# Router logits by held token columns, and three reorderings ahead of the experts

## What is computed

```python
def hierarchical_moe(h, rg_w, rg_b, re_w, re_b, e_gate, e_up, e_down):
    t = h.reshape(-1, D)
    g_prob = softmax(t @ rg_w + rg_b)                 # 4 groups
    g_val, g_idx = top_k(g_prob, 1)
    e_logits = (t @ re_w + re_b).reshape(-1, 4, 8)    # 8 experts in each group
    e_sel = take_along_axis(e_logits, g_idx)[:, 0]
    e_val, e_idx = top_k(softmax(e_sel), 2)
    ...
    for gi in range(4):
        a = einsum('td,edf->tef', t, e_gate[gi])
        u = einsum('td,edf->tef', t, e_up[gi])
        hid = silu(a) * u * combine[:, gi, :, None]
        out = out + einsum('tef,efd->td', hid, e_down[gi])
```

## Time and profile before

| | |
|---|---|
| time, median of 3 runs | 2110.43 us (2110.09 to 2112.68) |
| profiled execution: time | 2114.34 us |
| profiled execution: span, first to last instruction | 2112.5 us |
| TensorE busy, mean granted clock | 1849.6 us (88%), 0.925 |
| VectorE busy | 1330.5 us (63%) |
| ScalarE busy | 779.2 us (37%) |
| GpSimd busy | 496.4 us (23%) |
| routing stage, in the span | about 1764 to 1805 us |
| expert stage | about 1805 to 2093 us |

### The profile page before, as it was taken

How to read it: one execution, slowest core, us unless ns; L and a number is a source line. 1 busy time by engine, 2 the same in 40 slices (tenths; PEclk the granted TensorE clock), 3 DMA queues, 4 the chain that set the end, 5 groups by cost and what they waited for, 6 DMA issues and landing times. The chain is left out here.

```text
span 2112.5 us, 21287 instructions
## 1 busy us (share of the span) xinstructions
PE 1849.6 (88%) x8780; PEld 1447.2 (69%) x8780; DVE 1330.5 (63%) x1664; ACT 779.2 (37%) x994; POOL 496.4 (23%) x417
## 2 busy tenths in 40 slices
PE   4999878789699999699999996998688897789985
PEld 3778756677697888477888784776554574677774
DVE  3235588879545343566235455798978565798995
ACT  3343334332003123343123223324246433666663
POOL 1030066767242000110000001433200000544440
PEclk8999887789899999899999997999889998899997
DMA  6121020002001223134334341221110111989893
GB/s 224 62 80 61 20 80 0 1 21 85 16 2 60 80 100 126 54 140 163 148 147 180 140 159 41 85 100 60 60 60 1 40 40 48 358 341 349 338 352 148
DMA packets 37329, 241.35 MB, mean 114 GB/s; under 512 B 4192, under 2 KB 4704, under 8 KB 10736
## 3 DMA queue, kind: packets, MB, share of 16 engines
q1 hardware_dynamic: 23984, 147.69, 18.9%
q0 software_dynamic: 13248, 92.30, 11.4%
HBM read 228.39 MB, written 11.58 MB: 114 GB/s over the span
## 5 line engine op out<-in xcount | busy, mean ns | idle before, releaser
L336 PE MATMUL bank<-h_high,wsplit 128*128 128x512 f32 x992 | 323.4, 405 | 25.6 <-POOL wsplit L1339 8.6
L1339 DVE TENSOR_TENSOR wsplit<-ring,wsplit 128x2048 fp32r<-128x2048 f32 x77 | 177.4, 2304 | 182.0 <-ACT wsplit L821 181.9
L821 ACT ACTIVATE wsplit<-ring 128x2048 fp32r<-128x2048 f32 x98 | 186.9, 1907 | 212.3 <-PE bank L336 188.3
L336 PEld LDWEIGHTS bank<-h_high,wsplit 128*128 128x128 f32 x992 | 190.3, 192 | 79.9 <-POOL wsplit L1339 9.5
L336 PE MATMUL bank<-xn_high,wsplit 128*128 128x512 f32 (+1 forms) x832 | 219.9, 352 | 27.0 <-DVE wal_low L1390 18.5
L336 PE MATMUL bank<-h_low,wsplit 128*128 128x512 f32 x496 | 199.5, 402 | 0.0
L336 PEld LDWEIGHTS bank<-xn_high,wsplit 128*128 128x128 f32 x832 | 148.3, 194 | 49.3 <-issue 19.9
L336 PE MATMUL bank<-f_high,wsplit 128*128 128x512 f32 x512 | 166.3, 405 | 4.4 <-DVE f_low L1759 4.4
L2227 POOL TENSOR_TENSOR x<-x,z 128x512 f32<-128x512 f32 x8 | 12.8, 1594 | 598.8 <-DVE z L1697 598.8
L336 PE MATMUL bank<-xn_low,wsplit 128*128 128x512 f32 (+1 forms) x416 | 145.6, 350 | 0.0
L1799 DVE SCALAR_TENSOR_TENSOR conv<-conv_in,vecs,conv 128x512 f32<-128x512 f32 x120 | 140.5, 1171 | 4.3
(11 more groups left out here) (465 smaller groups left out, 3890.2 us busy)
## 6 DMA issues: line engine op xcount, KB each, us to landing
ring<-in_W SPq DMA_DIRECT2D x122, 1024.0 KB, 4.8
xslot<-zeros SPq DMA_DIRECT2D x7, 516.0 KB, 5.0
block<-xslot SPq DMA_DIRECT2D x7, 516.0 KB, 11.0
yslot<-block_out SPq DMA_DIRECT2D x7, 512.0 KB
x_in<-in_xT SPq DMA_DIRECT2D x4, 528.0 KB, 7.4
x<-in_xT SPq DMA_DIRECT2D x2, 1024.0 KB, 6.2
out_y<-h_tokens SPq DMA_DIRECT2D x4, 512.0 KB, 2.6
bc<-in_bc SPq DMA_DIRECT2D x1, 1024.0 KB, 4.7
```

Of the source, the lines that this page charges most:

```text
L336: return g.matmul(o, l, r, start=first, stop=last_, skip_group_check=True)
L821: g.activation(wst[:, side(n), 0, :], ringt[:, n % RING, :], ACT.Copy).then_inc(*a.sig(("high", n)))
L1339: g.tensor_tensor(wst[:, side(n), 1, :], ringt[:, n % RING, :], hi, SUB).then_inc(*t.sig(("low", n), ("released", n)))
```

## The change

Four edits; the rest of the program is as it was.

The router product is turned round: 128 token columns of `HB` are the held weights and the 36 router columns move, for each of 8 feature tiles and 4 groups of tokens. The result stands in one bank as 128 tokens x 144, where the bias add reads it. The copy to `logits_t`, its buffer `LT` and the four transposes are gone.

On ScalarE all `h_tokens` copies stand ahead of the two exponentials. On ScalarE and on VectorE, tiles 0 and 1 are split ahead of `turn_block(0)`.

```diff
-            b = fresh("logits")
+            b = fresh("logits_t")
             p.wait_ge(route_landed, 32)
             for k in range(8):
                 p.wait_ge(*at("hb", k))
-                t = mm(b[0:36, :], RW[:, k, :], HB[:, k, :], k == 0, k == 7)
-            t.then_inc(*p.sig(("logits",)))
-            banks.close("logits")
-            b = fresh("logits_t")
-            p.wait_ge(*at("lt"))
-            for m in range(4):
-                t = g.transpose(b[:, 36 * m:36 * m + 36], LT[0:36, 128 * m:128 * m + 128], ident[0:36, 0:36])
+                for m in range(4):
+                    t = mm(b[:, 36 * m:36 * m + 36], HB[:, k, 128 * m:128 * m + 128], RW[:, k, :], k == 0 and m == 0, k == 7)
             t.then_inc(*p.sig(("logits_t",)))
...
             a.wait_ge(*at("end", "mix2", "pe"))
-            tokens("ht", HT, 0)
-            tokens("ht", HT, 1)
+            for m in range(4):
+                tokens("ht", HT, m)
             a.wait_ge(*at("exp_in"))
             g.activation(RO["eg"], RO["eg"], ACT.Exp).then_inc(*a.sig())
             g.activation(RO["exx"], RO["exx"], ACT.Exp).then_inc(*a.sig(("exps",)))
-            tokens("ht", HT, 2)
-            tokens("ht", HT, 3)
...
+            for _ in range(2):
+                part(upto[0])
+                upto[0] += 1
             turn_block(0)
...
-            v.wait_ge(*at("logits"))
-            g.tensor_copy(LT[0:36, :], banks.at("logits")[0:36, :]).then_inc(*v.sig(("free", "logits"), ("lt",)))
...
+            for _ in range(2):
+                part(upto[0])
+                upto[0] += 1
             turn_block(0)
```

More of the change, by code:

```diff
@@ L271, in program @@
         HB, RW, MCT = tile("hb", 0, 8, 512), tile("router", 10240, 8, 36), tile("moe_cst", 10528, MC)
-        LT, L, HT = tile("logits_t", 10688, 512), tile("logits", 11200, 4, 36), tile("h_tokens", 11344, 4, ROW)
+        L, HT = tile("logits", 11200, 4, 36), tile("h_tokens", 11344, 4, ROW)
         RT, IX = tile("routing", 15472, 640), tile("indices", 16112, NB * 12 + 4).bitcast(I32)
```

## The result

The changed kernel takes 2118.1 us (median of 10 runs, 2113.74 to 2123.07), the kernel before 2109.85 (10 runs, 2107.74 to 2113.64). The ratio is 1.0040 with a 95% interval from 1.0028 to 1.0053, so it is 8.4 us slower (5.9 to 11.2). The forecast was 5.4 us slower, or 2115.8 us with a range of 2109.5 to 2120.5, and slower by more than 0.2% was the likeliest case. The time lies in the range, the cost was larger than forecast, and two of the terms were wrong.

A forecast was written before the change was run, and what follows sets the result against it. The prediction saw a serial routing path, then an expert-stage start ended by a gathered weight tile's landing. 3.4 (router product) + 0 (copies) + 2.0 (tiles) = +5.4 us, or 2115.8 us for the median; range 2109.5 to 2120.5.

The forecast's parts named there:

- Part 1: Router product turned round: 64 passes at 0.216 us, clock 0.50 throughout, counting matmuls low too; VectorE goes on +3.4 us later.
- the forecast's upper bound: Router product: +4.3 us if the old product in other executions got its clock back in 4.1 us, not 5.8.
- The upper rival: Clock stays low through the row transposes and diagonal products behind the router product: 6.1 us more, 2121.9; chance 0.08.
- Part 2: h_tokens copies ahead of the exponentials on ScalarE: not last before the scatters, so no gain; cost nought, up to +0.5.
- Part 3: Two weight tiles ahead of the block's split: first product 3.1 us sooner, only more idle; +2.0 through the clock.
- the move doesn't touch that landing, so 1823.92 stays: Expert stage start: gathered weight tile still lands at 1818.28, so the first hidden transpose stays at 1823.92.
- The other term: TensorE idles 4.6 us instead of 1.48 ahead of the first hidden transpose, the clock drops: +2.0 us.

The follow-up runs named there:

- x1_router: Kernel before with only the router product turned round (36 moving columns), copies and weight tiles in the old order; ratio 1.0019, +4.0 us.
- x3_tiles: Kernel before with only weight tiles 0 and 1 split ahead of the block's split, on ScalarE and VectorE; ratio 1.0018, +3.8 us.
- x2_copies: Kernel before with only the h_tokens copies moved ahead of the exponentials; ratio 1.0008 (0.9996 to 1.0019), +1.7 us.
- x9: Changed kernel with the row copies and exponentials back in the old order; ratio 1.0034 against the kernel before, +7.2 us.
- x4_tiles_split: Kernel before with two weight tiles ahead of the block's split on ScalarE but only one on VectorE; ratio 0.9997, -0.6 us.
- x6_warm: Kernel before with 12 unread passes of constants by 512 columns ahead of the router product's waits; ratio 0.9988, -2.5 us.
- x12: Changed kernel with 128 moving columns per router pass instead of 36, 92 of them unread; ratio 1.0035 against the kernel before, +7.4 us.
- x11_keep_all: Kernel before plus turned 128-column product, early h_tokens copies, unread passes ahead of router product, six block boundaries and diagonal products; ratio 1.0066, +13.9 us.
- x7_wide_warm: Kernel before with the router product turned round, 128 moving columns per pass, and 12 unread passes ahead of it; 2108.81 us, ratio 0.9982.

## Why the prediction was right, and where it wasn't

**Part 1 was right, in its mechanism and its size.** The step was: 64 passes of 0.216 us at 0.50 to the end, counting at the low level behind them, +3.4. After shows 0.216 a pass, 0.50 throughout, the add 13.88 behind the start (forecast 14.1) and +3.1. x1_router gives it alone. What was luck is the execution of before that it is set against: against the old product of x3_tiles the same step is +4.7, above the +4.3 that was the forecast's upper bound. The row that carried it was the nearest in moving columns, against a rule that goes by busy time. The upper rival, a low clock through all the transposes, didn't come: the clock rose among the 24 + 32 transposes behind the counting matmuls, 0.50, 0.80 and 1.00 in the three stretches from 1783 to 1792. What the prediction said no row was pure for, that transposes raise the clock, is shown there. The Trainium skill's page "TensorE: Matmul & The Clock Gate", section "Part 4: PE-mode transpose", says that they don't count as activity; these rows differ from it, and they decide.

**Part 2 failed at the step "gains nothing, cost nought".** It asked only who was waiting for the copies. It took "the x_tokens copies come sooner" for harmless and didn't follow it to TensorE: sooner copies free the banks sooner, TensorE's transposes end sooner, and the gap ahead of the diagonal products, which depend on VectorE, gets longer by it (2.55 in after, 4.19 in x2_copies, 1.23 in x1_router). The clock falls in it. That cost 1.7 (x2_copies against before) and 1.8 (the changed kernel against x9) in the time from the step behind the count to the block load, and 1.3 and 1.5 by the whole stages. By time alone neither is told from nothing, and the old order fell into the same low clock in two of the ten profiled executions that have it (x4_tiles_split and x6_warm), the new one in all three without passes to keep it.

**Part 3 was right in direction and wrong in one step.** The step "the move doesn't touch that landing, so 1823.92 stays" failed. Measured from the block's transposes the hidden ones came 1.7 later, since the subtraction of tile 1, which now runs beside the first gather, holds GpSimd's issue (x3_tiles against x4_tiles_split, and the table of the rests: 2.0 with the transfer taken out). A row of before had shown it, which I didn't read: the gather of tile 5 beside VectorE's subtraction.

```profile
1805.84 0.98 POOL L2263 DMA_INDIRECT ring<-in_wmoe,indices  x1 [7.55 <-DMA block<-xslot]
...
1809.64 3.02 POOL L2263 DMA_INDIRECT slot<-in_wmoe,indices  x1 [0.30 <-issue]
```

The other term, the clock behind the longer idle time, was forecast at 2.0 with 4.6 of idle. After has 4.92 of idle and 1.4 of loss; x3_tiles 1.4, x12 1.5, x4_tiles_split 2.3, x9 2.6. The size was near, and in after below the 1.6 that the forecast had as its least. A shorter idle time can be enough: in x11_keep_all, without the tiles ahead, the clock fell behind 2.22 of idle and the stretch took 15.99.

**The sum.** Forecast 3.4 + 0 + 2.0 = 5.4. Measured in the stage 3.1 + 1.7 + 1.7 + 1.4 - 0.1 = 7.8, and 8.4 by time. The terms that the forecast had wrong are the nought of Part 2, which measured 1.7, and the nought for the landing in Part 3, which measured 1.7; the clock term came out 0.6 lower. One agreement was chance: the block load was forecast near 1805 and came at 1804.80, but the product had started 1.8 sooner; from its start the load was 1.4 later than forecast (37.34 against 35.9), and that was Part 2.

## What to carry to other kernels

When the operands of a product change places, look at the moving columns of a pass: here 36 left the clock at 0.50 through 14 us of full work, 128 raised it, and padding with columns that nobody reads cost next to nothing (0.115 us a pass at 1.00, against 0.108 for 64 columns in the earlier trace rows). Before moving a step ahead of a transfer's issue, look for two-operand SBUF work on VectorE that now lies beside GpSimd's issues, and put only so much ahead as ends before they start. Follow a step that comes sooner through to the engine it releases: if that engine then runs dry, the clock can take back more than the step gave; and work put in to fill an idle stretch must not need what ends it.

## What the runs showed of the hardware that I had not expected

- An indirect gather of GpSimd that is issued while VectorE subtracts with both operands in SBUF ends 0.81 to 0.87 us behind the end of that subtraction: 1.92, 2.31, 2.81 and 2.99 us long in place of 0.98. One issued 0.4 before the subtraction began took 0.94 (at 1824.49 in after).
- A clock that is up can fall under full work: 64 passes of 36 columns that began at 1.00 took 12.18 us, of 128 columns 7.38.
- The clock rose from 0.50 to 1.00 while nothing but transposes ran (behind 1784 in after, 1.00 from 1789 on).
- The spread of this kernel's executions (2107.7 to 2113.6 before) is probably in part that of the block boundaries, which differ from profile to profile: the same 3.06 us of idle cost 1.6 us of clock in some and nothing in others. Why in one and not in the other stays open.
- Not tried: x7_wide_warm with the tiles split as in x4_tiles_split.
